# Cumulative sums of the stick-breaking heads: from three full-precision products to rounded-format products of a split operand

## The reference

```python
z = einsum('bhqd,bshd->bhqs', qb, k) * (HEAD_DIM_C ** -0.5)
before = kpos[None, :] < qpos[:, None]
log_keep = where(before, log_sigmoid(-z), 0.0)
stick = lax.cumsum(log_keep, axis=3, reverse=True) - log_keep
w = where(before, exp(log_sigmoid(z) + stick), 0.0)
out = einsum('bhqs,bshd->bqhd', w, v)
```

## Time and profile before

| | |
|---|---|
| three runs, median (lowest to highest) | 2127.47 us (2126.68 to 2127.59) |
| profiled execution, device time | 2127.58 us |
| its span in the profile | 2125.8 us |
| TensorE busy | 2100.9 us (99%) |
| VectorE busy | 1233.2 us (58%) |
| ScalarE busy | 1079.1 us (51%) |
| share of TensorE in the chain that ended last | 98% |
| mean granted TensorE clock | 0.997 |

### The profile page before, as it was taken

The page is one execution under the profiler, slowest core; times in us unless marked ns, Lnnn a source line. Parts: engine busy times, 40 slices in busy tenths (PEclk is TensorE's granted clock), DMA queues, the critical chain, the costliest instruction groups (busy, mean ns, idle before and its releaser), DMA issues.

```text
span 2125.8 us, 30062 instructions
## 1 busy us (share of the span) xinstructions
PE 2100.9 (99%) x10823; PEld 1787.8 (84%) x10823; DVE 1233.2 (58%) x1565; ACT 1079.1 (51%) x1578; POOL 50.4 (2%) x87
## 2 busy tenths in 40 slices
PE   8999999999999999999999999999999999999997
PEld 7888888888888888888888888888888888888886
DVE  5687656546555655655545544566556545655654
ACT  6578555435534544554444555455435434534554
POOL 3121000000000000000000000000000000000000
PEclk9999999999999999999999999999999999999999
DMA  8454655665666566655666544655566666666664
GB/s 249 144 164 139 195 181 188 191 195 179 198 196 189 181 199 193 188 188 188 188 190 189 181 134 129 198 179 189 194 191 188 191 195 188 184 200 180 197 193 133
DMA packets 297983, 390.97 MB, mean 184 GB/s; under 512 B 12288, under 2 KB 204960, under 8 KB 297760
## 3 DMA queue, kind: packets, MB, share of 16 engines
q1 hardware_dynamic: 296816, 385.98, 58.2%
q0 software_dynamic: 944, 3.70, 0.6%
q10 hardware_dynamic: 128, 0.03, 0.0%
HBM read 387.53 MB, written 2.12 MB: 183 GB/s over the span
## 4 chain that ended last, share of the span: by engine, by line
PE 98%; ACT 1%; DVE 0%; POOL 0%; issue 0%; DMA 0%; ACTq 0%; POOLq 0%; DVEq 0%
PE psum L394 48%; PE psum L419 15%; PE psum L420 15%; PE psum L421 15%; PE psum L453 1%; PE psum L1147 0%; POOL relu_sq L917 0%; PE psum L1173 0%; PE psum L859 0%; PE psum L1189 0%; PE psum L997 0%; DMA mix<-in_rel_bias_dram 0%; PE psum L856 0%; PE psum L1175 0%; PE psum L1191 0%
## 5 line engine op out<-in xcount | busy, mean ns | idle before, releaser
L373 DVE TENSOR_TENSOR w_split<-raw,w_split 128x1024 fp32r<-128x1024 f32 x728 | 887.5, 1229 | 751.2 <-ACT w_split L366 750.9
L366 ACT ACTIVATE w_split<-raw 128x1024 fp32r<-128x1024 f32 x728 | 764.5, 1058 | 818.4 <-PE psum L421 488.9
L394 PE MATMUL psum<-hg_op,w_split 128*128 128x512 f32 (+1 forms) x6016 | 1063.1, 338 | 1.3 <-DVE hg_op L470 1.3
L394 PEld LDWEIGHTS psum<-hg_op,w_split 128*128 128x128 f32 x6016 | 917.4, 189 | 136.4 <-issue 3.3
L419 PE MATMUL psum<-w_split,ff_op 128*128 128x512 f32 x1280 | 499.3, 390 | 0.0
L421 PE MATMUL psum<-w_split,ff_op 128*128 128x512 f32 x1280 | 498.1, 389 | 0.0
L420 PE MATMUL psum<-w_split,ff_op 128*128 128x512 f32 x1280 | 498.0, 389 | 0.0
L421 PEld LDWEIGHTS psum<-w_split,ff_op 128*128 128x128 f32 x1280 | 240.3, 188 | 50.3
L419 PEld LDWEIGHTS psum<-w_split,ff_op 128*128 128x128 f32 x1280 | 240.3, 188 | 49.4
L420 PEld LDWEIGHTS psum<-w_split,ff_op 128*128 128x128 f32 x1280 | 240.3, 188 | 48.9
L434 ACT ACTIVATE cross<-psum 128x256 f32<-128x256 f32 x188 | 66.0, 377 | 61.8 <-PE psum L394 61.6
(11 more groups left out here) (151 smaller groups left out, 624.7 us busy)
## 6 DMA issues: line engine op xcount, KB each, us to landing
raw<-in_w_up_dram SPq DMA_DIRECT2D x256, 512.0 KB, 3.8
raw<-in_w_down_dram SPq DMA_DIRECT2D x256, 512.0 KB, 3.8
raw<-in_odd_w_in_dram SPq DMA_DIRECT2D x96, 512.0 KB, 4.1
raw<-in_even_w_in_dram SPq DMA_DIRECT2D x56, 512.0 KB, 4.0
raw<-in_even_w_out_dram SPq DMA_DIRECT2D x32, 512.0 KB, 3.8
raw<-in_odd_w_out_dram SPq DMA_DIRECT2D x32, 512.0 KB, 3.8
h<-in_x_dram SPq DMA_DIRECT2D x4, 512.0 KB, 7.5
mix<-rel_dram POOLq DMA_DIRECT2D x4, 512.0 KB, 6.1
```

What stands on the lines that cost most here:

```text
L366: act.activation(w_hi[:, slot], raw[:, rs], ACT.Copy).then_inc(hi_done, 1)
L373: dve.tensor_tensor(w_lo[:, slot], raw[:, rs], w_hi[:, slot].bitcast(F32), ALU.subtract).then_inc(lo_done, 1)
L394: ins = nc.tensor.matmul(o, l, r, start=(k == 0 and n == 0), stop=(k == KT - 1 and n == 1), skip_group_check=True)
```

## The change

- The 256 columns of tri hold the triangle and the block of -1 side by side. A new function tri_act copies them on ScalarE once, at key 67, to the rounded format (tri_r); both values, 0 and -1, are exact in it.
- sp_hi_act (ScalarE, at k + 2) rounds a head's softplus (384 columns) to sp_hi; sp_lo_dve (VectorE, at k + 2) subtracts it and writes the rest, rounded, to sp_lo.
- cum_pe, still at k + 2, waits for sp_lo and issues four products in the rounded format: triangle times sp_hi and times sp_lo over all 384 columns, and the block of -1 times the last 128 columns of each.
- softplus_act of head n waits for sp_lo of head n - 2 where it waited for that head's cum; sp_hi_act takes over the wait for the cum.
- A buffer of 2048 columns in the rounded format holds sp_hi, sp_lo and tri_r, and in the even layer the bias tables, which leave the shared buffer mix.

```diff
+        def tri_act(act):
+            act.wait_ge(stick_const, 2)
+            act.activation(tri_r, tri, ACT.Copy).then_inc(tri_done, 1)
+
+        def sp_hi_act(act, n):
+            act.wait_ge(sb_sp, n + 1)
+            if n >= 2:
+                act.wait_ge(sb_cum, n - 1)
+            act.activation(sp_hi[:, n % 2], sp[:, n % 2], ACT.Copy).then_inc(sb_sphi, 1)
+
+        def sp_lo_dve(dve, n):
+            dve.wait_ge(sb_sphi, n + 1)
+            dve.tensor_tensor(sp_lo[:, n % 2], sp[:, n % 2], sp_hi[:, n % 2].bitcast(F32),
+                              ALU.subtract).then_inc(sb_splo, 1)
+
         def cum_pe(pe, n):
-            pe.wait_ge(sb_sp, n + 1)
+            pe.wait_ge(sb_splo, n + 1)
             if n == 0:
-                pe.wait_ge(stick_const, 2)
-            bank, s = 4 + n % 2, sp[:, n % 2]
-
-            nc.tensor.matmul(psum[:, bank, 0:S], ntri, s[:, 0:S], start=False, stop=False, skip_group_check=True)
-            nc.tensor.matmul(psum[:, bank, P:S], nones, s[:, S:384], start=False, stop=False, skip_group_check=True)
-            nc.tensor.matmul(psum[:, bank, S:384], ntri, s[:, S:384], start=False, stop=True,
-                             skip_group_check=True).then_inc(sb_cum, 1)
+                pe.wait_ge(tri_done, 1)
+            bank = 4 + n % 2
+            for s in (sp_hi[:, n % 2], sp_lo[:, n % 2]):
+                nc.tensor.matmul(psum[:, bank, 0:384], tri_r[:, 0], s, start=False, stop=False, skip_group_check=True)
+            for s, last in ((sp_hi[:, n % 2], False), (sp_lo[:, n % 2], True)):
+                ins = nc.tensor.matmul(psum[:, bank, P:S], tri_r[:, 1], s[:, S:384], start=False, stop=last,
+                                       skip_group_check=True)
+            ins.then_inc(sb_cum, 1)
...
+        at_key("act", ODD + ODD_KEYS[0] - 2, tri_act)
         for n, k in enumerate(ODD_KEYS):
             for d, which, fn in ((5, "act", out_act), (5, "dve", out_dve), (3, "act", weight_act), (0, "pe", z_pe),
-                                 (1, "act", softplus_act), (1, "dve", softplus_dve), (2, "pe", cum_pe),
+                                 (1, "act", softplus_act), (1, "dve", softplus_dve), (2, "act", sp_hi_act), (2, "dve", sp_lo_dve),
+                                 (2, "pe", cum_pe),
                                  (4, "pe", av_pe)):
                 at_key(which, ODD + k + d, fn, n)
```

More of the change, by code:

```diff
@@ L44 @@
 SUB_KT = 4
-MIX = 14 * 1024 + 520
+MIX = 12 * 1024 + 520
 AHEAD = 3
@@ L162, in build @@
         mix = sb("mix", [P, MIX])
+        early_r = sb("early_r", [P, 2048], F32R)
         psum = ctx.enter_context(nc.psum_tensor("psum", [P, 8, 512], F32))
@@ L180, in build @@
         prob_t, at = carve(at, [3, 512])
-        bias, at = carve(at, [2, 4, 2 * P])
+        bias = early_r[:].bitcast(F32).rearrange("p (b c s) -> p b c s", b=2, c=4)
         gate_w, at = carve(at, [2, NL, P])
@@ L204, in build @@
         assert at <= MIX
-        ntri, at = carve(at, [P])
-        nones, at = carve(at, [P])
+        tri, at = carve(at, [2, P])
         assert at <= MIX
+        ntri, nones = tri[:, 0], tri[:, 1]
+        sp_hi = early_r[:, 0:768].rearrange("p (b s) -> p b s", b=2)
+        sp_lo = early_r[:, 768:1536].rearrange("p (b s) -> p b s", b=2)
+        tri_r = early_r[:, 1536:1792].rearrange("p (a s) -> p a s", a=2)
         zmask = sb("zmask", [P, P], BF16)
@@ L277, in build @@
         sb_z, sb_ln, sb_sp, sb_cum, sb_w = sem("sb_z"), sem("sb_ln"), sem("sb_sp"), sem("sb_cum"), sem("sb_w")
+        sb_sphi, sb_splo, tri_done = sem("sb_sphi"), sem("sb_splo"), sem("tri_done")
         sb_av, sb_hi = sem("sb_av"), sem("sb_hi")
@@ L1153, in softplus_act @@
             if n >= 2:
-                act.wait_ge(sb_cum, n - 1)
+                act.wait_ge(sb_splo, n - 1)
             s = sp[:, n % 2]
```

## The result

The changed kernel takes 2129.9 us (median of 20 runs, 2128.9 to 2132.1) and the kernel before 2127.3 us (20 runs, 2126.0 to 2128.3). The ratio is 1.0014, with a 95% interval of 1.0008 to 1.0021: slower by 0.14%, clear of the noise, but less than the 0.2% that the prediction set as its bound for a difference. The forecast was 2130.3 us with a range of 2128.4 to 2133.9.

The account below looks back on a forecast made before the run. TensorE, busy 99% of the span, was taken as the bound. Shorter sums (-4.7 us) and waits at four heads (+7.4) gave +2.7 on 2127.58, so 2130.3 us, range 2128.4 to 2133.9.

Parts of the forecast that it names:

- Gain of a sum: TensorE's cumulative sum per head: 0.57 us instead of 0.88, 0.31 less, with 0.11 us per rounded product over 128 columns.
- Heads that keep the gain: All but head 13, whose shorter sum becomes wait at head 15's scores: 15 x 0.31 = 4.7 us gained.
- Inner heads: Sums of 12 heads: av covers sp_lo, margin 0.07 to 0.16 us; cost nothing, at most 1.2 us.
- Last sub-steps: Heads 0, 4, 8, 12: sp_lo stands behind the leave, so TensorE waits; 2.33 + 3 x 1.68 = 7.4 us.
- Sum: Whole kernel: -4.7 + 7.4 = +2.7 us, giving 2130.3 us, chance 0.48.
- The clock: Rival: TensorE's clock falls to half in the new waits; one fall gives 2131.9 us, two 2133.5; chance 0.22.

Follow-up runs that it names:

- all heads early: Changed kernel with every head's rounding and rest (sp_hi_act, sp_lo_dve) one key earlier, at k + 1: 2122.7 us, ratio 0.9979.
- head 0 alone late: Changed kernel with rounding and rest one key earlier for every head except head 0, which stays behind the leave: 2126.2 us, ratio 0.9994.
- one more shift: Changed kernel with every head's rounding and rest one key earlier, plus head 13's weights (Exp) one key earlier: 2121.9 us, ratio 0.9976.

## Why the prediction was right

- **Gain of a sum.** 0.31 us predicted, 0.34 measured (7.94 to 7.60). The piece without a row of its own, 0.11 for a product over 128 columns, measured 0.108. The new sum itself was forecast at 0.57 us: it takes 0.60 behind an av and 0.53 at head 0 with all heads early, where nothing stands in front of it. Behind an av the gain has a part that I didn't see: from the av's last instruction to the sum TensorE now takes 0.14 us instead of 0.22.
- **Heads that keep the gain.** Fifteen, as said: the scores of head 15 now wait 0.32 us idle more for the weights of head 13, which swallows the gain of head 13's sum. From that sum to those scores it is 1.84 us before (1312.80 to 1314.64) and after (1317.22 to 1319.06).
- **Inner heads.** No wait, as said. The margin was larger than 0.07 to 0.16: from the end of the rest to a product that waited for it there are 0.05 us (head 0, 1215.07 to 1215.12), where I had taken 0.12 to 0.15 from the earlier trace rows. Taking the av away cost 0.42 a head (0.6 said), so of its 0.65 us some 0.23 are margin, and it is indeed the cover.
- **Last sub-steps.** Head 0: 2.33 us predicted. The changed kernel runs 0.15 ahead there (L1151 at 1206.48, L1145 before at 1206.63), so the sum would start at 12.89 past 1200 and starts at 15.12: 2.23. Head 4: 1.68 predicted, 1.68 measured. With the heads moved ahead of the leave the waits are gone and the kernel is 7 us faster than the changed one, so this step was the cause, and it was sized nearly rightly (7.4 us predicted, 7.3 by these rows).
- **Sum.** +2.7 predicted without a fall of the clock. By the measured terms, 2.23 + 3 x 1.68 - 15 x 0.34 = +2.2, and the stretch of the heads shows +2.3; the lower group lies +1.8 over before, the upper one +4.05. The median of all is +2.6, close to the forecast partly by luck: with eleven runs in the lower group and nine in the upper one it is the upper edge of the lower group (2129.9), and two falls more among the 20 would have put it above 2131.
- **The clock.** This is the step that was sized too low. I gave a fall a chance of 0.22. By the groups it came in 9 of 20 and 4 of 11 executions, and in 6 of 11 of the kernel with head 0 alone late. Its price was right, 1.55 predicted and 1.62 measured. The mechanism and the place were named, but two of my reasons don't hold. I compared head 0's delay of 2.33 us with an idle time of 2.17; in idle time head 0's wait is 2.07, the shorter of the two. And the wait of 1.30 us in the earlier trace rows says nothing about a fall: TensorE wasn't at full speed in front of it (eight transposes take 1.97 us there and 1.03 later, at 15.04), and in eight of the eleven profiles the products behind this wait are slow. The waits of 1.35 to 1.42 us with full speed on both sides are the evidence that I lacked. The sum with one fall (2131.9) was put just above the bound of 2131.7; the upper group lies at 2131.35, under it, since the forecast without a fall (2130.3) was 1.2 above the lower group. A mechanism that falls or not by execution belongs in the forecast as a second group of times and not as a rival.

## What to carry to other kernels

Where a transformation adds a step between a producer and the bound engine, look up for each instance what stands in front of it on its own engine's queue. The same two instructions cost nothing in twelve heads and 7.3 us in four, since in those four they stood behind work that waits for the bound engine's last product. One key earlier they cost one wait more, 0.5 us at the scores of the heads 14 and 15, and the change pays 4.4 us, with one more shift 5.1.

A wait that is taken away can have covered a later one: trace the next close place before counting the whole of it.

## What the runs showed of the hardware

- A wait of TensorE of 2.07 us idle was followed by a stretch at half clock in some executions and not in others of the same program, and within one execution behind three such waits and not behind a fourth. Early in the run, waits of 2.17 to 2.26 us had it behind them in all three profiles that have such a wait. Waits of 1.35 to 1.42 us idle never showed it. A fall cost 1.6 us.
- A rounded product over 128 columns costs 0.108 us, as much as one pass of float32 at that width. The format takes one pass there where float32 takes two, and a value split in two parts takes both of them back. The gain of the change is in the products over 384 columns: 0.32 us for a float32 pass (0.65 for two in the joined product) and about 0.16 for a rounded one, an estimate from (0.88 - 0.34 - 2 x 0.108) / 2.
- Joining two float32 products over 256 and 128 columns into one over 384 changed nothing (ratio 1.0000).
